# A hybrid mLSTM and attention block on one core: Z records dealt out unevenly, a weight load moved, and the mLSTM branch's output as block pairs

## What is computed

```python
h = rms_norm(x, g_norm) * (1.0 + scale) + shift
xa, va, oa, za, ia, fa, qa, ka, vat, zb, ga, gb = split(h @ w_in)
# four mLSTM heads of width 256
y_m = (h_m * silu(za)) @ w_out_mlstm                 # 1024 x 1024 @ 1024 x 1024
# twelve attention heads in three dilation groups, joined to four
y_a = (o_a * silu(zb)) @ w_out_attn                  # 1024 x 512 @ 512 x 1024
merged = sigmoid(ga) * y_m + sigmoid(gb) * y_a
x = x + gate * (merged @ w_out)
return rms_norm(x, g_final)
```

## Time and profile before

| | us |
|---|---|
| median of 3 runs (lowest to highest) | 1370.97 (1370.72 to 1371.75) |
| the profiled execution's own time | 1371.11 |
| its span | 1369.3 |
| outside the span | 1.8 |
| PE busy, share of the span | 1345.7, 98% |
| DVE, ACT, POOL busy | 855.3, 580.1, 463.0 |

### The profile page before, as it was taken

The page is one execution under the profiler, slowest core; times in us unless marked ns, Lnnn a source line. Parts: engine busy times, 40 slices in busy tenths (PEclk is TensorE's granted clock), DMA queues, the critical chain, the costliest instruction groups (busy, mean ns, idle before and its releaser), DMA issues.

```text
span 1369.3 us, 17469 instructions
## 1 busy us (share of the span) xinstructions
PE 1345.7 (98%) x6453; PEld 1126.9 (82%) x6453; DVE 855.3 (62%) x1472; ACT 580.1 (42%) x1016; POOL 463.0 (34%) x298
## 2 busy tenths in 40 slices
PE   8999999999999999999999999999999999999998
PEld 6888888888888888888898788889878887888886
DVE  7988766573745444535368757866875766434586
ACT  7663353343444344332545446354545534111122
POOL 0096555554545555543002200210120022222551
PEclk9999999999999999999999999999999999999999
DMA  8522323323234343337231841553172165453543
GB/s 316 196 82 95 132 99 123 123 93 115 101 123 139 123 143 134 139 112 228 73 83 48 231 93 32 161 148 94 48 227 67 33 241 205 128 187 140 173 138 108
DMA packets 65454, 180.52 MB, mean 132 GB/s; under 512 B 22001, under 2 KB 22129, under 8 KB 63318
## 3 DMA queue, kind: packets, MB, share of 16 engines
q1 hardware_dynamic: 61082, 166.64, 36.9%
q10 hardware_dynamic: 3168, 8.70, 1.9%
q0 software_dynamic: 1120, 4.06, 1.0%
HBM read 132.49 MB, written 46.89 MB: 131 GB/s over the span
## 4 chain that ended last, share of the span: by engine, by line
PE 87%; DVE 6%; ACT 3%; DMA 2%; issue 1%; SPq 0%; POOL 0%; ACTq 0%; DVEq 0%
PE banks L592 23%; PE banks L594 23%; PE banks L593 23%; PE banks L1265 4%; PE banks L1390 2%; PE banks L1400 2%; PE banks L1350 2%; PE banks L1356 2%; DMA wraw<-in_w_all 1%; PE banks L1339 1%; PE banks L1348 1%; PE banks L1409 1%; PE banks L584 1%; PE banks L556 1%; PE banks L1378 1%
## 5 line engine op out<-in xcount | busy, mean ns | idle before, releaser
L1248 POOL TENSOR_TENSOR wlo<-wraw,whi 128x1024 fp32r<-128x1024 f32 x28 | 72.1, 2575 | 436.5 <-ACT whi L1468 411.1
L718 POOL TENSOR_TENSOR wlo<-w_sum,whi 128x512 fp32r<-128x512 f32 x112 | 165.2, 1477 | 137.4 <-ACT whi L843 137.4
L592 PE MATMUL banks<-t_hi,whi 128*128 128x512 f32 x448 | 174.3, 389 | 0.0
L593 PE MATMUL banks<-t_lo,whi 128*128 128x512 f32 x448 | 174.3, 389 | 0.0
L594 PE MATMUL banks<-t_hi,wlo 128*128 128x512 f32 x448 | 174.3, 389 | 0.0
L989 DVE TENSOR_TENSOR c_sum<-c_sum,banks 128x512 f32<-128x512 f32 x196 | 134.4, 686 | 44.7 <-PE banks L594 30.6
L592 PE MATMUL banks<-h_hi,whi 128*128 128x512 f32 x416 | 162.0, 389 | 0.0
L594 PE MATMUL banks<-h_hi,wlo 128*128 128x512 f32 x416 | 161.9, 389 | 0.0
L593 PE MATMUL banks<-h_lo,whi 128*128 128x512 f32 x416 | 161.8, 389 | 0.0
L843 ACT ACTIVATE whi<-w_sum 128x512 fp32r<-128x512 f32 x112 | 70.5, 630 | 165.5 <-PE banks L594 100.7
L592 PE MATMUL banks<-whi,h_hi 128*128 128x512 f32 x256 | 100.2, 391 | 1.4 <-POOL wlo L1248 1.4
(11 more groups left out here) (374 smaller groups left out, 2904.8 us busy)
## 6 DMA issues: line engine op xcount, KB each, us to landing
wraw<-in_w_all SPq DMA_DIRECT2D x72, 512.0 KB, 4.3
raw<-in_w_all SPq DMA_DIRECT2D x28, 512.0 KB, 4.4
queries_keys<-fin SPq DMA_DIRECT2D x12, 1024.0 KB, 4.0
qa<-queries_keys SPq DMA_DIRECT2D x12, 768.0 KB, 13.7
s_wada<-in_w_ada_cols SPq DMA_DIRECT2D x16, 512.0 KB, 8.2
attn_values<-fin SPq DMA_DIRECT2D x6, 1024.0 KB, 4.0
tn<-attn_values SPq DMA_DIRECT2D x12, 512.0 KB, 10.1
sig_c<-merge_gates SPq DMA_DIRECT2D x6, 1024.0 KB, 6.4
```

The source lines that it names most:

```text
L592: t_.matmul(out, w_hi, x_hi, start=first, stop=False)
L593: t_.matmul(out, w_hi, x_lo, start=False, stop=False)
L718: nc.gpsimd.tensor_tensor(wlo4[:, o % 4, :], source(r, j), whi4[:, o % 4, :].bitcast(F32), subtract).then_inc(s_split, 1)
L1248: nc.gpsimd.tensor_tensor(to, wraw[:, q % 2, :], hi.bitcast(F32), ALU.subtract).then_inc(w_split, 1)
```

## The change

Three edits.

**Z records.** The 96 records of a head's Z tiles are dealt out over the same 24 points in uneven parts, and ScalarE's `keep` moves to the point in which its group is formed, with one of the four behind `mixing`. 13 records now stand ahead of `head_q` instead of 8.

**Weight load.** In `turn_stats` the next head's load of p = 0 stands ahead of the wait for `cw_done`.

**mLSTM branch.** um is made as four block pairs (28 to 31) like those of `blocks`, with 4 x 7 x 12 records instead of 8 x 48. The seven activation factors are quarters of `um` or differences of them, each 128 partitions x 2048 elements, prepared by VectorE (differences and lo parts) and ScalarE (hi parts). um tiles 0 to 5 are loaded from ScalarE's queue at the end of the last head, and 6 and 7 come from SBUF. `gate(m)` multiplies the joined tiles in SBUF by their gate. Then ua follows for all eight tiles, and `merge_tile` adds into the same tiles, which stay in SBUF: no store and no reload. GpSimd splits them there. The row loads of `finish` still wait for `BRANCH_DONE`, which now is the end of the last ua group; before, the last ua tile still followed it. `out_high` and `out_low` are in another order and partly later.

```diff
-    PARTS_OF, RECORDS = 6, 4
-    POINTS = 2 * PARTS_OF * (MAIN - ZA)
+    RECORDS = 3 * KT
+    SIZES = (6, 7, 4, 4) + 6 * (3,) + 9 * (4,) + (5, 4, 4, 4, 4)
+    ENDS = list(itertools.accumulate(SIZES))
+    POINTS = len(SIZES)
...
+            for u in range(POINTS):
+                for record in range(ENDS[u] - SIZES[u], ENDS[u]):
+                    project(record)
+                if u == 1:
+                    head_q()
...
+                mixing(u)
...
+            for u in range(POINTS):                       # ScalarE
+                if u == formed_at(ZA, 0):                 # u = 4
+                    keep(ZA, 0)
+                if u == formed_at(ZA, 1):                 # u = 12
+                    keep(ZA, 1)
+                    next_high(ZA + 2)
+                if u == formed_at(ZA + 1, 1):             # u = 23
+                    keep(ZA + 1, 1)
+                    next_high(ZA + 3)
...
+                mixing(u)
+                if u == formed_at(ZA + 1, 0):             # u = 18
+                    keep(ZA + 1, 0)
...
         def turn_stats(i):
-            for q in range(2):
+            for q in range(2) if i < HEADS - 1 else ():
...
             sp.dma_start(ct[:]...).then_inc(ct_in, 16)
+            if i + 1 < HEADS:
+                load(HEAD0 + (i + 1) * CHUNKS + AHEAD)
+            for q in range(2) if i == HEADS - 1 else ():
+                sp.wait_ge(um_done, 2 * HEADS - 1 + q)
+                sp.dma_start(T["um_raw"][:, KT - 2 + q, :], xc[:, q, :]).then_inc(T["tile_in"][KT - 2 + q], 16)
             sp.wait_ge(cw_done, i + 1)
...
+        act.wait_ge(out_turned, 4 * HEADS)                # ScalarE, end of mix
+        for q in range(2):
+            act.wait_ge(um_out[q], 16 * HEADS)
+        for k in range(KT - 2):
+            act.dma_start(T["um_raw"][:, k, :], um_d[k // 2, k % 2]).then_inc(T["tile_in"][k], 16)
...
+        T["shared"]["group_exp"](HEADS - 1)               # ScalarE in merge
+        first_sigmoid(0, 0, 1)
+        first_sigmoid(0, 1, 1)
+        branch_high(up_left_hi, up_left[0], range(KH))
+        pair_high(0)
+        sum_high(5)
+        first_sigmoid(0, 0, 0)
+        pair_high(1)
+        first_sigmoid(0, 1, 0)
+        branch_high(low_left_hi, low_left[0], range(KH, KT))
+        first_sigmoid(1, 0, 1)
+        first_sigmoid(1, 1, 1)
+        weight_high(TOTAL)
+        weight_high(TOTAL + 1)
+        first_sigmoid(1, 0, 0)
+        act.wait_ge(ua_out, 16 * HEADS + 16)
+        sum_high(6)
+        sum_high(4)
+        first_sigmoid(1, 1, 0)
+        weight_high(TOTAL + 2)
+        weight_high(TOTAL + 3)
+        for o in range(TOTAL, WITH_BRANCH):
...
+            if o + 4 < WITH_BRANCH:
+                weight_high(o + 4)
+            if o == TOTAL:
+                sum_high(7)
+            if o == TOTAL + 1:
+                branch_high(low_right_hi, low_right[0], range(KH, KT))
...
+        T["shared"]["weigh_groups"](HEADS - 1)            # VectorE in merge
+        branch_rows(range(KH))
+        dve.wait_ge(pv_kept, 12 * HEADS + 1)
+        difference(5, up_right, up_left[0])
+        low(1, up_left[0])
+        branch_rows(range(KH, KT))
+        difference(6, low_right[0], bt_raw[5], 5)
+        low(5, bt_raw[5])
+        for part in ("scale_two", "join_two", "join_third", "gate_attn"):
+            T["shared"][part](HEADS - 1)
+        dve.wait_ge(T["ua_done"], 2 * HEADS + 1)
+        weight_sums(PAIRS)
+        difference(4, low_left[0], bt_raw[6], 6)
+        low(2, low_left[0])
+        low(4, bt_raw[4])
+        low(6, bt_raw[6])
+        difference(7, low_right[0], up_right)
+        low(7, bt_raw[7])
+        low(3, low_right[0])
+        for r in BRANCH_PAIRS:
+            if r + 1 in BRANCH_PAIRS:
+                weight_sums(r + 1)
+            else:
+                for k in range(HEADS):
+                    attn_low(k)
+            join(r)
+            for j in range(2):
+                gate(2 * (r - PAIRS) + j)
...
+        pool.wait_ge(merged_half, merged(KT - 1, 0))      # GpSimd in finish: tiles 0 to 6 merged
+        split(0, slice(0, KT - 1), 1).then_inc(m_part, 1)
```

More of the change, by code:

```diff
@@ L1216, in sync @@
             for p in range(CHUNKS):
-                load(HEAD0 + i * CHUNKS + p + AHEAD)
+                if p or not i:
+                    load(HEAD0 + i * CHUNKS + p + AHEAD)
                 if p == 3:
@@ L1429, in tensor @@
             fold_weights()
[L1430 to L1439, removed]
+            for u in range(POINTS):
[3 more added lines that the diff above has]
+                    head_q()
+                if (i, u) == (0, 2):
+                    pe.wait_ge(decays_in, 32)
+                    t_.transpose(M1[:, 0:P], gr[:], ident[:]).then_inc(hc_turned, 1)
+                mixing(u)
     def scalar(act):
@@ new lines, in product @@
+        def product(r, j):
+            o = at_product(r, j)
+            bank_free(o)
+            pe.wait_ge(s_split, o + 1)
+            if r == PAIRS:
+                pe.wait_ge(t_lo_done, low_count(j))
+            hi, lo = factors[j]
+            for k in range(KH):
+                cols = slice(k * P, (k + 1) * P)
+                mm = three_pass(t_, bank(r, j), whi4[:, o % 4, cols], wlo4[:, o % 4, cols], hi[:, k, :], lo[:, k, :],
+                                k == 0, k == KH - 1)
+            mm.then_inc(gprod, 1)
@@ L2081, in vector, with branch_rows, difference, low @@
         step = T["shared"]["step"]
-        def split_low(k):
+        def branch_rows(ks):
+            for k in ks:
+                dve.wait_ge(tile_in[k], 32)
+        def difference(j, x, y, first=None):
+            if first is not None:
+                dve.wait_ge(t_raw, raw_count(first))
+            v.tensor_tensor(bt_raw[j], x, y, ALU.subtract).then_inc(t_raw, 1)
+        def low(j, raw_):
+            hi, lo = factors[j]
+            dve.wait_ge(t_hi_done, high_count(j))
+            v.tensor_tensor(lo, raw_, f(hi), ALU.subtract).then_inc(t_lo_done, 1)
@@ new lines, in plus, with join @@
+        def plus(r, name, out, x, j):
+            dve.wait_ge(gprod, 1 + at_product(r, j))
+            dve.wait_ge(part_added, added_part(r, name) - 1)
+            v.tensor_tensor(out, x, bank(r, j), ALU.add).then_inc(part_added, 1)
+        def join(r):
+            c11, c12, c21, c22 = (umo[:, 2 * (r - PAIRS) + j, part] for j in range(2) for part in (LEFT, RIGHT))
+            dve.wait_ge(first_kept, r + 1)
+            plus(r, "u2", c21, c11, 6)
+            plus(r, "u4", c12, c21, 5)
+            plus(r, "c11", c11, c11, 2)
+            plus(r, "c22", c22, c12, 7)
+            plus(r, "v", c21, c21, 7)
+            plus(r, "c21", c21, c21, 4)
+            plus(r, "c12", c12, c12, 3)
@@ L2208, in tensor @@
+        for t in range(1, NCH):
+            if t > 1:
+                pool.wait_ge(prod, 2 * t - 2)
+            split(t, slice(0, KT), t + 2).then_inc(m_split, 1)
     def tensor(pe):
```

518 lines of the change are left out of this document (294 added, 224 removed).

## The result

The changed kernel took 1373.74 us, the kernel before 1371.75 us beside it on the same chip: ratio 1.0021 (95% interval 1.0014 to 1.0028), 2.9 us slower. The forecast was 1360.3, and the result is outside its range of 1354.5 to 1366. So a forecast gain of 10.8 us became a loss of 2.9, 13.7 us apart. The loss is 0.2% of the time, small but clear of noise. The profiled execution has a span of 1371.9 (1369.3 before), and PE's last record starts at 1364.89 (1362.45 before). From here on all moments are those of profiled executions, and all ratios are against the kernel before, run beside.

What follows compares the result with a forecast made beforehand. PE was taken as the bound, busy 98% of the span: records times 0.2276 us plus pauses. Terms -10.9 - 3.2 - 2.0 - 1.3 + 4.1 + 2.5 = -10.8 took 1371.1 to 1360.3 us, range 1354.5 to 1366.

Steps and rivals of the forecast that it cites:

- 1 fewer records: um in the mLSTM branch: 336 PE records instead of 384, 48 fewer at 0.2276 us each, -10.9 us.
- 2 Z records: Heads: pause at `head_q` filled, lead of 1.37 less `keep` of 0.57 gives 0.80 us per head, -3.2 us in all.
- 3 weight load: Second and fourth heads: SyncE issues the weight load some 10 us earlier, so waits of 1.24 and 0.74 go, -2.0 us.
- 4 um_lo's wait: First branch tile: PE's waits for um_lo go because those operations no longer exist, -1.3 us.
- 5 preparation: First block pairs of the branch: VectorE and GpSimd add up, making products 4, 6, 7, 3 and next pair's first late, +4.1 us.
- 6 into finish: Step from ua into finish: split of tiles 0.8 us late, row loads for `gate_sum` 1.7 us late, +2.5 us.
- Rival C: Heads: the Z edit gives nothing, through thinned points waiting or the norm chain taking all; +3.2 us, 1363.5 us; 8%.
- rival A: First branch pair: `ct` waits for most of 3 MB of um tiles, landing at T+13.5; 3.7 us more, 1364.0 us; 17%.
- signs named for being wrong: `ua_done` far from T+36, PE standing at plain gate weights, or ua's tiles waiting for merges.
- B: Less new pause: VectorE and GpSimd overlap or order is luckier, finish cheaper, `keep` partly hidden; 1354.2 us; 15%.
- D: Branch: last activation factor over 14.9 us after PE's wish, `sum_high(7)` holding ScalarE; slower, about 1372 to 1376 us; 3%.

## Why the prediction was wrong

Each term against what the runs and traces show for it:

| step | forecast | measured | from |
|---|---|---|---|
| 1 fewer records | -10.9 | -10.9 | 6405 for 6453 |
| 2 Z records | -3.2 | +3.5 | 4 x (121.27 - 120.39) |
| 3 weight load | -2.0 | -2.1 | three intervals, run alone (by its ratio -1.5) |
| 4 um_lo's wait | -1.3 | -1.3 | the operations are gone |
| 5 preparation | +4.1 | +7.2 | 0.88 + 6.34 |
| 6 into finish | +2.5 | +6.4 | 94.8 - 89.0, and 0.6 lost among ua's 192 records ahead of it (44.16 for 43.53) |
| sum | -10.8 | +2.8 | ratio: +2.9; PE's last record in the two traces: +2.4 |

**Step 2 failed, and it alone is half of the miss (6.7 us).** Filling the pause at `head_q` worked (the wait is gone), and the `keep` cost 0.48 where I had charged 0.57. Of the lead of 1.37 some 1.16 came: with only the first group a point earlier, `hnb` of the last-but-one step is that much sooner in its head than with the even records. What failed is the sentence that `next_high(ZA + 2)` one point later feeds the next head only, a term put at nothing. True for its data, not for the engines: the `keep` and the copy moved ahead of another `hin` on ScalarE (0.66), and the split behind the copy moved onto another part of VectorE's chain (1.21); together they cost 1.57 per head. I had written the rule down in step 5, that the two don't overlap where both read SBUF only, and applied it to 2048-element operations; it holds a 128x1 operation just as long. The same slip is in the walk of the thin points, where I looked at when `hnb` was ready and not at what GpSimd was doing. By the run that moves nothing but this one record, a head then gains 0.69 over the even distribution, near the 0.80 forecast. Rival C saw a Z edit that gives nothing at 8%; an edit that costs 0.88 per head was outside my bounds, which went to 0 and not beyond, though an added collision was a reason to.

The Trainium skill (SBUF — State Buffer, Who interferes with whom) says that a VectorE instruction with two SBUF inputs contends with a GpSimd one that reads SBUF, and calls the ports that both share an exclusive lock. The trace agrees: L1733, with one tensor input, takes 0.15 us in the middle of GpSimd's split, and L1734 behind it, with two, ends 0.02 us after it.

**Step 6: a size.** For the split ahead of the first block I had charged 0.8; PE lost 0.2 there, two steps of 0.34 at 1270.11. The row loads cost 3.9 for 1.7 (the terms given, 7.9 - 6.3, make 1.6). I had all the bytes in the sum, but charged x with half of its 2.5 us; the run that holds x back takes 3.4 off `gf`, more than all of x's own time. I had nothing for the clock: a pause of this length had no example in the trace of before, whose page has 9 in every slice. It adds 1.8 in `gate_sum` here, and 0.1 in the run with the even Z records, whose pause was nearly as long (3.6).

**Step 5: rival A came true, at half its price.** `ct` landed at T+13.0; A had said T+13.5. With `ct` ahead of the um tiles the stage gets 2.2 us shorter, not 3.7, since the tiles are then late by nearly as much: A had taken them to be there. The walk itself held up: with the early `ct` the five pauses behind the first are 0.45, 0.48, 1.43, 0.46 and 0.35, against 0.5, 0.8, 1.5, 0.8 and 0.5 in the forecast. The first, at product 2 (0.88 to 2.17), was not in it; it hangs on ScalarE's order, as the two runs with the weights ahead showed, where it is gone. Two of the signs named for being wrong came: attention was done at T+39.7 for T+36, and PE stood 0.9 us at a plain gate weight.

**Rivals.** B (less pause) did not come; C was right about the place and wrong about the sign; D's chain never was near 14.9 us late. The slower result came by three middling errors of one direction (6.7, 3.1 and 3.9 us), two of them outside their bounds (step 2: 0; step 6: 4) and the third near its own (step 5: 8). My 3% for slower counted one mechanism only.

## What to carry to other kernels

When an edit moves an operation by one point, follow every engine that it wakes, and lay that engine's time over what then runs beside it: here one matmul record in another place was worth 1.57 us per head, by way of ScalarE and GpSimd. Where loads move to a moment at which others start, add up all their bytes ahead of the last one needed; and if a consumer can come later (`gate_sum`) or a load that nobody needs yet can be held back (x), either alone gave 4.5 us. Where pauses can't be removed, look at the clock before joining them: here several short ones were cheaper than one long one.

## What the hardware showed that I had not expected

- A VectorE operation on 128x1 elements with two SBUF inputs took 1.43 us for 0.22 because GpSimd was in the middle of a split of 2.38.
- After PE pauses of up to 2.2 us the next records keep their pace of 0.23. After pauses of 2.7, 4.7 and 5.8 they were 0.43 apart for a while, after one of 3.9 `gate_sum` took twice its time, and stretches of 4 us in the profile show a granted clock of 0.50 to 0.89: some 1.5 to 2.8 us lost on top of the pause. The 2.8 are of the kernel with um behind `ct`: 30 records from `gate_sum` on take 10.43 us, 9.44 in the changed kernel and 7.66 before. It is not the length alone: after one of 2.9 (plain gate, late `gate_sum` kernel) and one of 3.6 (ahead of `gate_sum`, even Z records) the pace stayed, while after one of 3.5 at the same place (only the first group a point earlier) it fell. The Trainium skill (TensorE: Matmul & The Clock Gate, The HAM clock gate) has the clock fall to half after idleness; the traces agree on the two levels.
- A load of 24 KB took 9.6 us to land (11.6 in another execution) beside 3 MB that were issued before it on another queue, and 3.4 when they were issued behind it on its own queue.
